# Two-layer diffusion trunk: where early gate weights are rounded, how gate steps are dealt over the attention groups, and where branch C's head means stand

## The reference, cut to what matters

```
z = h @ p['w_in']                                  # 7456 columns
a_q, a_k, a_v, c_q, ..., merge_logits = split(z)   # merge_logits: 4 * 1024 columns
y_a = attend(...)                                  # 4 heads, 64 wide
o1, o2 = attend(...), attend(...)                  # 4 heads, two 32-wide maps each
y_c = rms_norm(o1 - lam * o2, p['c_subln_g']) * (1 - lam_init)
y_b, y_d                                           # two chunked recurrences (HGRN2, GLA)
proj  = einsum('btnw,nwd->btnd', branches, p['w_branch'])
gates = sigmoid(merge_logits)
mixed = sum(gates * proj, axis=2) @ p['w_out']
x = x + g1 * mixed                                 # then the ConvFFN
```

## Time and profile before

| | |
|---|---|
| median of 3 runs (lowest, highest) | 2498.03 us (2496.0, 2498.76) |
| profiled execution, its time | 2499.66 us |
| its span, first to last instruction | 2497.9 us |
| VectorE, ScalarE busy | 1488.9 us (60%), 1015.7 us (41%) |
| mean granted TensorE clock | 0.981 of full speed |
| attention of layer 0, from first gate step to the first merge product | 281.1 to 437.6 us |

### The profile page before, as it was taken

How to read it: one execution, slowest core, us unless ns; L and a number is a source line. 1 busy time by engine, 2 the same in 40 slices (tenths; PEclk the granted TensorE clock), 3 DMA queues, 4 the chain that set the end, 5 groups by cost and what they waited for, 6 DMA issues and landing times. The chain is left out here.

```text
span 2497.9 us, 49608 instructions
## 1 busy us (share of the span) xinstructions
PE 2387.4 (96%) x21594; PEld 2221.7 (89%) x21594; DVE 1488.9 (60%) x2274; ACT 1015.7 (41%) x1408; POOL 305.6 (12%) x203
## 2 busy tenths in 40 slices
PE   5999998899999999999989999979999999999998
PEld 4999776889999899999989996768999989999998
DVE  4134476876745688883241436768775657888621
ACT  4245455222243455561143536542222545554410
POOL 0000000000000445540000000000000005555100
PEclk8999998899999999999999999989999999999999
DMA  8545110212236233333244331102222542332321
GB/s 273 189 164 180 44 46 22 54 50 59 62 121 206 67 85 85 85 118 88 76 143 125 117 105 51 49 27 54 55 61 86 175 133 73 90 90 77 101 81 65
DMA packets 326510, 239.32 MB, mean 96 GB/s; under 512 B 18273, under 2 KB 317345, under 8 KB 325025
## 3 DMA queue, kind: packets, MB, share of 16 engines
q1 hardware_dynamic: 317584, 211.32, 28.9%
q10 hardware_dynamic: 8720, 24.99, 2.9%
HBM read 220.68 MB, written 15.60 MB: 95 GB/s over the span
## 5 line engine op out<-in xcount | busy, mean ns | idle before, releaser
L790 PE MATMUL PS<-HH_split,WHI_split 128*128 128x320 f32 x1952 | 618.8, 317 | 12.9 <-DVE HL_split L2015 10.4
L792 PE MATMUL PS<-HH_split,RING_split 128*128 128x320 f32 x1920 | 596.5, 311 | 0.0
L791 PE MATMUL PS<-HL_split,WHI_split 128*128 128x320 f32 x1760 | 548.1, 311 | 0.0
L2040 DVE TENSOR_TENSOR RING_split<-RING,WHI_split 128x1024 fp32r<-128x1024 f32 (+2 forms) x166 | 237.2, 1431 | 268.7 <-ACT WHI_split L1708 180.7
L790 PEld LDWEIGHTS PS<-HH_split,WHI_split 128*128 128x128 f32 x1952 | 370.7, 190 | 25.6 <-issue 15.2
L792 PEld LDWEIGHTS PS<-HH_split,RING_split 128*128 128x128 f32 x1920 | 363.5, 189 | 0.0
L791 PEld LDWEIGHTS PS<-HL_split,WHI_split 128*128 128x128 f32 x1760 | 335.0, 190 | 0.3
L791 PE MATMUL PS<-ZT_split,WHI_split 128*128 128x320 f32 x1032 | 319.3, 309 | 0.0
L740 POOL TENSOR_TENSOR BIG<-HH_split,HL_split 128x640 f32<-128x640 f32 x8 | 14.3, 1823 | 1786.1 <-DVE HL_split L2012 1786.1
L2047 DVE TENSOR_TENSOR RING_split<-RING,WHI_split 128x1024 fp32r<-128x1024 f32 x52 | 62.2, 1223 | 226.9 <-ACT WHI_split L1406 226.6
L791 PEld LDWEIGHTS PS<-ZT_split,WHI_split 128*128 128x128 f32 x1032 | 194.2, 188 | 0.0
(11 more groups left out here) (320 smaller groups left out, 5495.5 us busy)
## 6 DMA issues: line engine op xcount, KB each, us to landing
RING<-in_w_in SPq DMA_DIRECT2D x96, 512.0 KB, 4.0
RING<-in_w_up SPq DMA_DIRECT2D x88, 512.0 KB, 5.0
RING<-in_w_ada SPq DMA_DIRECT2D x80, 512.0 KB, 6.1
RING<-in_w_down SPq DMA_DIRECT2D x32, 384.0 KB, 3.5
RING<-in_w_in SPq DMA_DIRECT2D x40, 256.0 KB, 3.4
RING<-in_w_down SPq DMA_DIRECT2D x32, 320.0 KB, 3.9
RING<-in_w_out SPq DMA_DIRECT2D x16, 512.0 KB, 4.6
ZT<-in_w_ada SPq DMA_DIRECT2D x8, 1024.0 KB, 9.1
```

The lines of the kernel that those rows point to most:

```text
L790: release(pe.matmul(out, w_hi, hi[:, a:b], start=begin, stop=False), fresh and a == 0)
L791: pe.matmul(out, w_hi, lo[:, a:b], start=False, stop=False)
L792: ins = pe.matmul(out, w_lo, hi[:, a:b], start=False, stop=end)
L2040: nv.tensor_tensor(rest, value, as_f32(hi), ALU.subtract).then_inc(lo_made, 1)
```

## The change

Rounded weights of the early gates go into the second half of the ring slot that holds the raw ones (`W_GATE`), so no two neighbouring gates share a buffer. ScalarE rounds gate n+1 ahead of the copy of gate n's first half, not its second, and VectorE makes its rest half a gate sooner; for gate 1 that is ahead of the first maxima. `GATE_FILL` becomes a list by group: 1 and 2 steps in groups 0 to 23, 1 and 1 in the next eight, none in the last. The first merge unit is rounded at group 28 (before: 26), its rest made at 29 (before: 28). The two means of branch C move from behind the first level's products into the first merge gate, behind parts 1 and 5 (counted from 0), and the rounding of branch A's outputs and the norms move with them.

```diff
-GATE_FILL, FIRST_FILL = ((1, 1), (1, 5), (0, 2), (4, 2)), 8
+FIRST_FILL = 8
+GATE_FILL = ((1, 2),) * 24 + ((1, 1),) * 8 + ((0, 0),)
...
-    return min(2 * N_EARLY, (FIRST_FILL + sum(sum(GATE_FILL[i % 4]) for i in range(g))) // KT)
+    return min(2 * N_EARLY, (FIRST_FILL + sum(sum(GATE_FILL[i]) for i in range(g))) // KT)
...
+        W_GATE = [RING_R[:, b, 1024:2048] for b in range(N_SLOT)]
-        MIX_AT = 4 * NS + 2
+        MIX_AT = NG - 2
...
-                        w_hi, w_lo = tiles_of(W_EARLY), raw(RING_R, EARLY + n, 0, P, P, KT)
+                        w_hi, w_lo = tiles_of(W_GATE[(EARLY + n) % N_SLOT]), raw(RING_R, EARLY + n, 0, P, P, KT)
...
-                    for _ in range(GATE_FILL[g % 4][n]):
+                    for _ in range(GATE_FILL[g][n]):
...
-                fill("start", 0)
+                for n in range(FILL[0]):
+                    next(parts)
+                    if n in (1, 5):
+                        mean_square_c(n // 4)
...
                             for e in range(2):
-                                if x == 0 and p == 0:
-                                    mean_square_c(e)
                                 fill(x, 2 * groups * p + h + e)
...
# ScalarE: early_unit writes W_GATE[(EARLY + n) % N_SLOT] instead of W_EARLY
-                        if h and n + 1 < N_EARLY:
+                        if h == 0 and n + 1 < N_EARLY:
                             early_unit(n + 1)
...
                 act.activation(YSQ, ZT[:, CQ, :], ACT.Square).then_inc(csq_ready, 1)
+                act.wait_ge(stored, l * N_STORE + N_STORE)
+                for k in range(2):
+                    round_y(0, k)
                 act.wait_ge(cms_ready, l * 2 + 1)
                 inv_root(YRSTD, pair(1)[:, 0:T]).then_inc(crstd_ready, 1)
                 act.activation(YSQ, ZT[:, CQ + 1, :], ACT.Square).then_inc(csq_ready, 1)
-                act.wait_ge(stored, l * N_STORE + N_STORE)
-                for k in range(2):
-                    round_y(0, k)
                 mix_unit(1)
...
# VectorE
-                    if g == MIX_AT + 2:
+                    if g == MIX_AT + 1:
                         first_mix_lo()
-                    while early < N_EARLY and 2 * early <= halves_before(g - 1):
+                    while early < N_EARLY and 2 * early - 1 <= halves_before(g - 1):
...
                         # between the two products KM and QM of the first level
+                        if x == 0 and m == 0:
+                            norm_c(0)
+                            for k in range(2):
+                                y_rest(0, k)
...
                         if x == 0 and m == 0:
-                            for k in range(2):
-                                y_rest(0, k)
-                            norm_c(0)
                             mix_lo_unit(1)
+                            norm_c(1)
...
-                        if x == 0 and m == 0:
-                            norm_c(1)
```

More of the change, by code:

```diff
@@ L202 @@
 NG = NT * NS
-GATE_FILL, FIRST_FILL = ((1, 1), (1, 5), (0, 2), (4, 2)), 8
+FIRST_FILL = 8
+GATE_FILL = ((1, 2),) * 24 + ((1, 1),) * 8 + ((0, 0),)
+assert FIRST_FILL + sum(map(sum, GATE_FILL)) == 16 * N_EARLY
 TURN0 = [8 * (g // NS) + (0, 2, 4, 5, 6, 7)[g % NS] for g in range(NG)] + [8 * NT]
@@ L1526, in early_unit @@
                     chunk_in(EARLY + n)
-                    act.activation(W_EARLY, RING[:, (EARLY + n) % N_SLOT, 0:1024], ACT.Copy).then_inc(hi_made, 1)
+                    act.activation(W_GATE[(EARLY + n) % N_SLOT], RING[:, (EARLY + n) % N_SLOT, 0:1024], ACT.Copy).then_inc(hi_made, 1)
                 early_unit(0)
@@ L1581, in first_mix_unit @@
                 def first_mix_unit():
-                    assert halves == 2 * N_EARLY
+                    assert halves >= 2 * N_EARLY - 3
                     chunk_in(MIX)
@@ L2128, in early_lo @@
                 def early_lo(n):
-                    lo(U_MIX + n, RING_R[:, (EARLY + n) % N_SLOT, 0:1024], RING[:, (EARLY + n) % N_SLOT, 0:1024], W_EARLY)
+                    lo(U_MIX + n, RING_R[:, (EARLY + n) % N_SLOT, 0:1024], RING[:, (EARLY + n) % N_SLOT, 0:1024], W_GATE[(EARLY + n) % N_SLOT])
                 early_lo(0)
```

## The result

The changed kernel takes 2527.85 us (median of 4 runs, 2525.33 to 2529.07), the kernel before 2497.41 in the runs beside them: a ratio of 1.012, 95% interval 1.0105 to 1.0134. It is 30.4 us slower. I had said 14 us slower, 2512, with 2528 as the upper end. The direction holds, and so do the halts that I named as its cause; what the low clock behind them costs does not, and the loss is more than twice what I forecast.

The account below looks back on a forecast made before the run. TensorE, busy 96% of the span, was taken as the bound, by its halts and low clock. Layer 0 6.4+4.8-5.5=+5.7, layer 1 6.4+4.8-3.3=+7.9, together +13.6 us: 2512 us, range 2498 to 2528.

Parts of the forecast that it names:

- The halts: Context groups 2, 5, 10, 13, 18, 21: gate steps wait for ScalarE's half copy; 42.7 us together, 29.7 without halts.
- The start: Attention's first groups: rounding gate 1 and its rest add 2.2 us; group 0 takes 7.0 us, group 1 5.9.
- The floor: Attention groups of the light kinds 1 and 5: the chain through the exponentials allows no less than 4.5 us a group.
- The clock: TensorE behind the halts: three falls to the low clock of 1.6 us, 4.8 a layer; bounds none and seven (11.2).
- rival B: Attention halts cost only their length, no low clock: +4.0 us, 2502 us; chance 0.16.
- the third rival: Rival C, the last of the three rivals, on TensorE's clock behind gaps: 2525 us; chance 0.12.
- Groups 24 to the merge and the means' stretch: Attention's end to second level: 21.0 us to the merge, then 14.8; 5.5 us less in layer 0, 3.3 in layer 1.
- Rival A: Context groups: even dealing works, nothing halts and no clock falls; -22.0 us in all, 2476 us; chance 0.15.
- Rival C: TensorE: every gap costs clock, seven falls a layer, merge starts slow; +13.6+12.8 us, 2525 us; chance 0.12.
- The range: Whole kernel: the terms' bounds were said to run from 2498 to 2528 us, with rival A left out.

Follow-up runs that it names:

- filled gaps: Changed kernel plus 92 useless matmuls a layer in the six halts, ScalarE rounding ahead of its wait for the half: 2501.30 us, 1.0004 to the kernel before.
- aligned halves: Changed kernel with steps spread to group 30, each half gate ending as a group's last step, gate 1 rounded one half later: 2467.54 us, 0.9878.
- two gaps filled: Changed kernel, ScalarE rounding ahead of its wait, useless matmuls only in the halts of groups 5 and 13: 2506.53 us, 1.0023 to the kernel before.
- control: Changed kernel with only ScalarE's rounding put ahead of its wait for the half, no extra matmuls: 2526.43 us, 1.0111 to the kernel before.

## Why the prediction was wrong, and what of it held

- **The halts** held: six a layer, in the groups named, by the cause named. Waits of 1.1 to 3.6 us; TensorE went on at +6.48 us in group 5 (forecast 6.55). The copy moved into the group took them away.
- **The start** held: group 0 7.11 us for 7.0, group 1 5.89 for 5.9. In layer 1 group 0 took 5.67, but behind slow first steps; group 1 began as late behind the first gate step (10.9 us).
- **The floor** of 4.5 held: groups 7, 17, 19 and 23 took 4.51, with TensorE waiting 0.78 for an exponential in each.
- **The clock is the step that failed**: "I count three falls of 1.6 us a layer: 4.8. Bounds: none, and seven (11.2)." Measured by the filled gaps it is 26.5 us in both layers; in the traces 14.2 in layer 0 and 12.5 in layer 1, both above even the upper bound. Count and price were both too low. There were four falls in layer 0 (behind the halts of groups 5, 10, 13 and 21) and five in layer 1 (also behind that of group 2). Against the filled kernel's groups they cost some 2.9 us each, from 1.6 to 4.6, not 1.6.
- I took the price from twelve matmuls in the earlier trace rows, and that reading was wrong as well. The clock was not back when they ended, at 459.1: it was granted 0.50 until 460.3, 4.7 us behind the gap's end, and the second level's 80 matmuls took 1.09 us in that row, for 0.88 at full clock. And one place is no bound for another: behind the halt of group 13 the clock stayed low for 10.6 us of work without a gap, and groups 14 and 22 lost 3.9 and 3.8 us each. Why it stayed low so much longer there, no run shows.
- That the low clock's excess (17 us) is as large as the whole miss (30.4-13.6=16.8) is luck: context groups and means' stretch gave 5.7 us more than forecast, and 3.5 us came outside the changed stretches.
- The page of the Trainium skill that I had weighed, "TensorE: Matmul & The Clock Gate", section "HAM oscillation — how this bites in real kernels", warns of long idle gaps. Gaps of 1.5 to 2.2 us brought falls here too, though not each time, and the measurement decides. Short halts at no cost in clock are rival B; I had put the third rival beside that page by mistake.
- **Groups 24 to the merge and the means' stretch** held roughly: 20.1 us for 21.0, then 12.8 for 14.8. Together -8.4 and -6.2 where I had -5.5 and -3.3. The clock was up from the start (1.00), and VectorE was indeed what came late next: at 471.19 TensorE waits 0.64 for it, and VectorE's first key sum stood until 460.41, 2.1 us behind the merge's first product (forecast 3.9), as the last logits landed sooner.
- **Rival A** (no halts) fell with the six waits. Its number, 2476, rests on a slip: 29.7 us for the six groups puts group 21 at the floor of 4.5, where its kind takes 5.93, so A is 2479. The idea itself is worth at least that: with aligned halves 2467.54. **Rival B** (halts at their length only) is what the filled gaps made, 2501.30 for its 2502; the closeness is partly luck, since the larger gain from group 24 on and the unexplained rest cancel there too. **Rival C** (every gap costs clock, 2525) came nearest to the time, though with fewer and dearer falls than it said, and with the clock up at the merge (1.00), where it had it low.
- **The range** did not follow from its terms. With no falls and 17 us to the merge they give 2494, with seven falls and 27 us 2536; I wrote 2498 to 2528.

The terms in one line, for both layers, measured and in brackets forecast: halts, start and floors less the steps moved out, at full clock, +13.7 (12.8); low clock +26.7 (9.6); from group 24 to the second level -14.5 (-8.8); outside these +3.5 (0). Together 29.4 (13.6), the difference of the spans.

## What to carry to other kernels

When filler work shares one buffer that another engine empties in a fixed place of its own list, deal it so that each fill of the buffer ends just ahead of that place; an even share per group is worth less than that alignment. Price a new wait on TensorE at twice: its length, and the matmuls that stand behind it at half the clock, which need not recover within a few us of steady work; the price of one fall read in one place is no bound for another. Where a halt can't be avoided, even useless matmuls in it can pay.

## What the runs showed of the hardware that I had not expected

- After a halt of 2.77 us TensorE ran at half pace for some 10 us without a gap (371.48 to 382.1); after one of 3.37 us in the kernel before it was back in 4.7 (460.4). After the halts of 1.50 and 1.10 in layer 0 no group behind them was slow (groups 3 and 19: 5.93 and 4.51); after the same 1.50 in layer 1 group 3 took 7.50.
- A fall can come after its gap has ended. Behind the halt of 1.73 us the waiting step still ran at full pace (clock 1.00 from 353.2 to 353.9), and the scores that followed fell to half pace (0.50 from 355 to 360). In the gap of 3.37 us the clock had fallen after some 1.2 us (1.00 to 453.5, then 0.50).
- 92 useless matmuls a layer, 11 us of TensorE's time by 3.58 us for 30, made the program 26.5 us faster.
- Executions of one kernel differ by their clock: of the ten runs with two gaps filled the fastest (2500.51 us) had a mean granted clock of 0.989, the slowest (2510.43) 0.983. Which gap brings a fall differs between the layers of one execution, and between the traces of the changed kernel and of the control, which have the same halts.
